# A two-block transformer forward pass on one core: a rebuilt front with one-number norms, row-wise memory and key/value products, and a new order of matmuls

## The reference, cut to what matters

```python
h = rmsnorm(x, norm_g)                               # per token
(a_q, a_ckv, i_q, i_k, i_w, a_gate, b_q, b_k, b_v, b_gate,
 c_q, c_gate, mix_gate) = split_cols(h @ w_in, IN_SIZES)
ckv = rmsnorm(a_ckv, kv_norm_g)                      # per token, width 256
a_k, a_v = split(ckv @ w_kv_up)
qa, ka = rmsnorm(a_q, q_norm_a), rmsnorm(a_k, k_norm_a)   # per token and head, 6 heads of 128
ik = layernorm(i_k, idx_k_ln_g, idx_k_ln_b)
oa = dsa_attention(qa, ka, va, iq, ik, iw, bias_a, topk) * silu(a_gate)
qb, kb = rmsnorm(b_q, q_norm_b), rmsnorm(b_k, k_norm_b)   # 12 and 2 heads of 64
ob = sliding_window_attention(qb, kb, vb, sinks_b, bias_b) * silu(b_gate)
m_k, m_v = split(rmsnorm(mem, mem_norm_g) @ w_mem_kv)
qc, kc = rmsnorm(c_q, q_norm_c), rmsnorm(m_k, k_norm_c)   # 4 heads of 128
oc = memory_attention(qc, kc, vc) * silu(c_gate)
x = x + (g_a*(oa@w_up_a) + g_b*(ob@w_up_b) + g_c*(oc@w_up_c)) @ w_o
# second block: rms_norm, w_in_2, pooling, conv, w_o_2, then square(relu(u @ w_up)) @ w_down
```

## Time and profile before

| | us |
|---|---|
| median of 3 runs | 2173.51 (2173.22 to 2175.52) |
| the profiled execution | 2172.68, span 2170.9 |
| TensorE matmuls busy | 2091.2 |
| TensorE weight loads busy | 1759.2 |
| VectorE busy | 1469.6 |
| ScalarE busy | 953.2 |
| GpSimd busy | 106.6 |
| chain that ended last: TensorE, VectorE, ScalarE | 89%, 7%, 2% of the span |

### The profile page before, as it was taken

The page is one execution under the profiler, slowest core; times in us unless marked ns, Lnnn a source line. Parts: engine busy times, 40 slices in busy tenths (PEclk is TensorE's granted clock), DMA queues, the critical chain, the costliest instruction groups (busy, mean ns, idle before and its releaser), DMA issues.

```text
span 2170.9 us, 29736 instructions
## 1 busy us (share of the span) xinstructions
PE 2091.2 (96%) x10683; PEld 1759.2 (81%) x10683; DVE 1469.6 (68%) x1877; ACT 953.2 (44%) x1185; POOL 106.6 (5%) x102
## 2 busy tenths in 40 slices
PE   6899999899999999999999999989999999999997
PEld 5777778777777888899878878878888888888886
DVE  6796886966676655567997757566556656645655
ACT  5443434545555444533444464454333333333343
POOL 4010010200100100001100000000000000000001
PEclk9999999999999999999999999999999999999998
DMA  7644555454655655555565646545565555556552
GB/s 242 196 123 127 165 155 166 138 171 161 192 165 180 231 190 182 180 169 171 164 194 190 189 147 233 192 145 186 192 194 184 188 194 181 191 194 193 184 194 87
DMA packets 272168, 386.59 MB, mean 178 GB/s; under 512 B 12247, under 2 KB 160565, under 8 KB 271527
## 3 DMA queue, kind: packets, MB, share of 16 engines
q1 hardware_dynamic: 267644, 370.91, 53.1%
q0 software_dynamic: 2208, 9.96, 1.3%
q10 hardware_dynamic: 2203, 4.23, 0.6%
HBM read 382.79 MB, written 2.13 MB: 177 GB/s over the span
## 4 chain that ended last, share of the span: by engine, by line
PE 89%; DVE 7%; ACT 2%; issue 1%; DMA 0%; SPq 0%; DVEq 0%; ACTq 0%
PE acc L492 17%; PE acc L494 17%; PE acc L493 17%; PE acc L513 17%; PE acc L512 8%; PE acc L505 2%; PE acc L503 2%; PE acc L504 2%; DVE w_low L444 2%; DVE rstd L1536 1%; PE acc L509 1%; PE aux L1218 1%; PE aux L1281 1%; ACT w_high L436 1%; PE acc L510 1%
## 5 line engine op out<-in xcount | busy, mean ns | idle before, releaser
L444 DVE TENSOR_TENSOR low_rows<-stage_rows,high_rows 128x1024 fp32r<-128x1024 f32 x416 | 512.3, 1235 | 398.4 <-ACT high_rows L436 394.5
L436 ACT ACTIVATE high_rows<-stage_rows 128x1024 fp32r<-128x1024 f32 x416 | 438.9, 1058 | 582.3 <-PE acc L494 547.7
L444 DVE TENSOR_TENSOR w_low<-stage,w_high 128x1024 fp32r<-128x1024 f32 (+1 forms) x294 | 357.1, 1223 | 231.0 <-ACT w_high L436 228.2
L436 ACT ACTIVATE w_high<-stage 128x1024 fp32r<-128x1024 f32 (+1 forms) x294 | 305.0, 1039 | 472.0 <-PE acc L513 364.3
L513 PE MATMUL acc<-u,w_high 128*128 128x512 f32 x960 | 342.4, 399 | 0.0
L512 PE MATMUL acc<-u,w_low 128*128 128x256 f32 x960 | 270.2, 281 | 0.0
L513 PE MATMUL acc<-hT,w_high 128*128 128x512 f32 x675 | 244.7, 400 | 0.0
L513 PEld LDWEIGHTS acc<-u,w_high 128*128 128x128 f32 x960 | 180.5, 188 | 41.8
L512 PE MATMUL acc<-hT,w_low 128*128 128x256 f32 x675 | 201.3, 298 | 3.9 <-DVE w_low L444 3.9
L492 PE MATMUL acc<-high_rows,f_pair 128*128 128x512 f32 x512 | 199.2, 389 | 0.0
L493 PE MATMUL acc<-low_rows,f_pair 128*128 128x512 f32 x512 | 199.2, 389 | 0.0
(11 more groups left out here) (359 smaller groups left out, 3521.5 us busy)
## 6 DMA issues: line engine op xcount, KB each, us to landing
stage_rows<-in_w_in SPq DMA_DIRECT2D x160, 512.0 KB, 3.6
stage<-in_w_in SPq DMA_DIRECT2D x136, 512.0 KB, 3.5
stage<-in_w_up SPq DMA_DIRECT2D x128, 512.0 KB, 3.9
stage_rows<-in_w_down SPq DMA_DIRECT2D x128, 512.0 KB, 4.3
stage_rows<-in_w_o SPq DMA_DIRECT2D x64, 512.0 KB, 3.5
stage<-in_w_mem_kv SPq DMA_DIRECT2D x16, 512.0 KB, 6.0
stage_rows<-in_w_pool_out SPq DMA_DIRECT2D x16, 512.0 KB, 3.5
stage_rows<-in_w_conv_out SPq DMA_DIRECT2D x16, 512.0 KB, 4.6
```

The lines of the kernel that those rows point to most:

```text
L436: act.activation(high[:, pr, 0:kt, 0:p.cols], src[:, slot, 0:kt, 0:p.cols], ACT.Copy).then_inc(high_done, 1)
L444: dve.tensor_tensor(low[:, pr, 0:kt, 0:p.cols], src[:, slot, 0:kt, 0:p.cols], high[:, pr, 0:kt, 0:p.cols].bitcast(F32), ALU.subtract).then ...
```

## The change

Five things are changed together.

1. `mem` and `x`. `mem_pair` and `hT` are made straight from `aux` (all four banks in turn): ScalarE writes the high part with the gain as scale (`high_unit`), VectorE the low part (`low_unit`). The first slab of `mem_kv` needs only unit 0; units 4 to 7 are turned beside slabs 0 to 3. Sums of squares are made by ScalarE from rows (`row_squares`, 2048 columns with an accumulator): `x` beside slabs 4 and 5, `mem` beside 7 and 12. `x` is scaled by VectorE in rows beside slabs 6 and 7, then turned beside slabs 8 to 11. SP loads `x` after slab 2 and the parameters after slab 4, and waits for a part of `mem` ahead of slab 1. The bias rows move from `mem_kv` to `early`, slabs 8 to 15.
2. `mem_kv`, `kv_up` and a new job `bkv` (key and value of the B heads) multiply by rows; ScalarE empties their banks with the norm of the token as scale. No value is turned any more; the keys are (`turn_keys`), after VectorE has scaled them (`scale_heads`).
3. Norms are one number per token and head (`rs`): sums by matmuls whose stationary operand is the squares and whose moving operand has one or two columns (`sum_steps`), or by ScalarE's accumulator (`head_squares`), then one `chain_var`, `chain_root`, `chain_inverse` for a batch. Query norms go into the logits, key and query gains into the turned keys.
4. The flips of the bias table move from `early` 7 to 15 to `late` 2 to 10.
5. By tiles, a group of four k does its low weights first, then its high weights.

The core of the diff:

```diff
@@ multiply
-                        both, a = p.rhs(k0 + k)
-                        if first:
-                            pe.matmul(bk, high, both, start=True, stop=False, skip_group_check=True)
-                            pe.matmul(bk[:, 0:T], low, a, start=False, stop=False, skip_group_check=True)
-                        else:
-                            pe.matmul(bk[:, 0:T], low, a, start=False, stop=False, skip_group_check=True)
-                            mm = pe.matmul(bk, high, both, start=False, stop=final, skip_group_check=True)
+                    opened = k0 == 0
+                    if opened:
+                        pe.matmul(bk, tile(w_high, 0), p.rhs(0)[0], start=True, stop=False, skip_group_check=True)
+                    for k in range(kt):
+                        pe.matmul(bk[:, 0:T], tile(w_low, k), p.rhs(k0 + k)[1], start=False, stop=False, skip_group_check=True)
+                    for k in range(1 if opened else 0, kt):
+                        mm = pe.matmul(bk, tile(w_high, k), p.rhs(k0 + k)[0], start=False, stop=last and k == kt - 1, skip_group_check=True)
@@ jobs
-            ("mem_kv", Job(4, [Part(A["w_mem_kv"], 0, full, rhs_of(mem_pair), ("pair_ready", 0))], 2)),
+            ("mem_kv", Job(2, [by_rows(A["w_mem_kv"], 0, [2] * 8, mem_pair, ("pair_ready", 0))], 2)),
-            ("kv_up", Job(6, [Part(A["w_kv_up"], 0, [2], rhs_of(ckv_pair), ("ckv_ready", 0))], 8)),
-            ("late", Job(14, [Part(A["w_in"], A_GATE, full, rhs_of(hT))], 2)),
+            ("kv_up", Job(3, [by_rows(A["w_kv_up"], 0, [2], ckv_pair, ("ckv_ready", 0))], 4)),
+            ("late", Job(6, [Part(A["w_in"], A_GATE, full, rhs_of(hT))], 2)),
+            ("bkv", Job(1, [Part(A["w_in"], B_KV_COL, full, None, rows=hT)], 2)),
+            ("late2", Job(7, [Part(A["w_in"], B_GATE_COL, full, rhs_of(hT))], 2)),
@@ steps
+        SQUARE_AT = {"early": {1: 0, 5: 1, 9: 2, 13: 3, 17: 4}, "late": {17: 5, 21: 6, 25: 7, 45: 8, 49: 9}}
+        FLIP_AT = 2
+        BIAS_AT = 8
-        SILU_AT = 52
+        SILU_AT = {48: 0, 50: 1, 52: 2}
@@ sync, the first slabs
+                    for n in range(2 * job.S):
+                        if n == 1:
+                            sp.wait_ge(s("mem_in1"), 16)
+                        load_slab(sp, job, 0, n // job.S, n % job.S)
+                        if n == 2:
+                            for c in range(4):
+                                cols = slice(c * 512, (c + 1) * 512)
+                                sp.dma_start(x_in[:, :, cols], xr[:, cols].rearrange("(t p) d -> p t d", p=P)).then_inc(s("x_in"), 16)
+                        if n == 4:
                             other_params()
@@ scalar
+            def high_unit(pair, gain, q, first):
+                act.wait_ge(s("turned_pe"), first + q + 1)
+                for a in range(2):
+                    k = 2 * q + a
+                    act.activation(pair[:, k, 0, :], aux[:, q % 4, a * T:(a + 1) * T], ACT.Copy, scale=column(gain, k)).then_inc(s("pair_high"), 1)
+            for q in range(4):
+                high_unit(mem_pair, "mem_norm_g", q, 0)
+                round_high(act, jobs["mem_kv"], 0, 0, q)
+            def beside_mem(n):  # parts
+                if n < 4:
+                    high_unit(mem_pair, "mem_norm_g", 4 + n, 0)
+                if n in (4, 5):
+                    row_squares(x_in, "x", n - 4, "input_squared")
+                if n == 6:
+                    chain_root(0)
+                if 8 <= n < 12:
+                    for q in (2 * (n - 8), 2 * (n - 8) + 1):
+                        high_unit(hT, "norm_g", q, 8)
+            def head_squares(kind, rows, width, t, h, total):
+                col = RS[kind] + t * total + h
+                if head_count[0]:
+                    act.wait_ge(s("head_squared"), head_count[0])
+                head_count[0] += 1
+                act.activation(junk_head[:, 0:width], rows[:, t, h * width:(h + 1) * width], ACT.Square, accum_out=sq[:, col:col + 1]).then_inc(s("head_squared"), 1)
+            def kv_body(i, u, part):
+                for t in range(2):
+                    act.activation(kv_rows[:, t, r * ROW:(r + 1) * ROW], banks[:, t, :], ACT.Copy, scale=rs_col("ckv", t)).then_inc(s("kv_rows"), 1)
@@ tensor
+                if 8 <= n < 12:
+                    if n == 8:
+                        pe.wait_ge(s("x_scaled"), 2)
+                        pe.wait_ge(s("params_copied"), 5)
+                    for q in (2 * (n - 8), 2 * (n - 8) + 1):
+                        turn_unit(x_in, q, 8)
+            def sum_steps(name, n):
+                i = stages(SQUARE_AT[name], n, 1)
+                kind, r = SQUARED[i]
+                pe.wait_ge(s("squared"), i + 1)
+                        else:
+                            c = base + t * (A_HEADS if kind == "aq" else C_HEADS) + 2 * r + a
+                            mm = pe.matmul(aux[:, 1, c:c + 1], v, ones[:, 0:1], start=True, stop=True)
+                if n == 4:
+                    pe.wait_ge(s("ik_diag"), 2)
+                if n in (5, 6):
+                    pe.wait_ge(s("ck_scaled"), 1)
@@ vector
+            def low_unit(pair, gain, q, first):
+                dve.wait_ge(s("pair_high"), 2 * (first + q) + 2)
+                for a in range(2):
+                    k = 2 * q + a
+                    link.put(dve.scalar_tensor_tensor(out=pair[:, k, 1, :], in0=aux[:, q % 4, a * T:(a + 1) * T], scalar=column(gain, k),
+                                                      in1=pair[:, k, 0, :].bitcast(F32), op0=ALU.mult, op1=ALU.subtract))
+            def beside_mem(n):  # parts
+                if n in (6, 7):
+                    if n == 6:
+                        chain_inverse(0)
+                    dve.tensor_scalar(x_in[:, n - 6, :], x_in[:, n - 6, :], rs_col("x", n - 6), None, ALU.mult).then_inc(s("x_scaled"), 1)
+                if n == 6:
+                    other_params()
+                if 9 <= n < 13:
+                    for q in (2 * (n - 9), 2 * (n - 9) + 1):
+                        low_unit(hT, "norm_g", q, 8)
```

More of the change, by code:

```diff
@@ L442, in subtract_low @@
             dve.wait_ge(high_done, n + 1)
-            src, high, low = (stage_rows, high_rows, low_rows) if p.rows else (stage, w_high, w_low)
+            src, high, low = (stage_rows, high_rows, low_rows) if p.by_rows else (stage, w_high, w_low)
             dve.tensor_tensor(low[:, pr, 0:kt, 0:p.cols], src[:, slot, 0:kt, 0:p.cols],
@@ L488, in multiply @@
                     first, final = k0 + k == 0, last and k == kt - 1
+                    high, low = (v[:, pr, k, 0:p.cols] for v in ((high_rows, low_rows) if p.by_rows else (w_high, w_low)))
                     for t in range(2):
-                        bk = acc[:, 2 * bank + t, :]
+                        bk = acc[:, 2 * bank + t, 0:p.cols]
                         x_high, x_low = (p.rows[:, k0 + k, half, t * P:(t + 1) * P] for half in range(2))
-                        pe.matmul(bk, x_high, high_rows[:, pr, k, :], start=first, stop=False)
@@ L493, in multiply, with tile @@
-                        pe.matmul(bk, x_high, low_rows[:, pr, k, :], start=False, stop=False)
-                        mm = pe.matmul(bk, x_low, high_rows[:, pr, k, :], start=False, stop=final)
+                        pe.matmul(bk, x_high, high, start=first, stop=False)
+                        pe.matmul(bk, x_high, low, start=False, stop=False)
+                        mm = pe.matmul(bk, x_low, high, start=False, stop=final)
                 for j in range(0 if p.rows else p.cols // P):
                     bk = acc[:, 2 * bank + j, :]
-                    for k in range(kt):
-                        first, final = k0 + k == 0, last and k == kt - 1
-                        high, low = (w[:, pr, k, j * P:(j + 1) * P] for w in (w_high, w_low))
-                        if p.width:
+                    def tile(w, k):
+                        return w[:, pr, k, j * P:(j + 1) * P]
@@ L501, in multiply @@
+                    if p.width:
+                        for k in range(kt):
+                            first, final = k0 + k == 0, last and k == kt - 1
                             a, b = p.rhs(k0 + k if p.stride else 2 * POOL_ORDER[u] + k)
                             dst = bk[:, 0:p.width]
-                            pe.matmul(dst, high, b, start=first, stop=False)
-                            pe.matmul(dst, low, a, start=False, stop=False)
-                            mm = pe.matmul(dst, high, a, start=False, stop=final)
@@ L754, in beside_mem @@
[L754 to L770 removed]
+                r = rstd[:, 0:T]
@@ L831, in silu_step, with bkv_body @@
+            def bkv_body(i, u, part):
+                banks, group = group_done(act, jobs["bkv"], 0, 0)
+                act.wait_ge(acc_free, 2 + group)
+                for t in range(2):
+                    act.activation(bkv[:, t, :], banks[:, t, 0:2 * P], ACT.Copy).then_inc(s("bkv_rows"), 1)
+                act.wait_ge(s("bkv_rows"), 2)
```

(8 more changed lines are left out.)

832 lines of the change are left out of this document (430 added, 402 removed).

## The result

The changed kernel takes 2118.47 us, median of 4 runs (2118.22 to 2118.83), the kernel before 2173.36 beside it: a ratio of 0.9747, 95% interval 0.973 to 0.9764. The profiled execution took 2118.83 us (span 2117.0), 53.9 less of span than before. The forecast was 2118.

What follows compares the result with a forecast made beforehand. TensorE is busy in 96% of the span, so only less TensorE work or fewer and shorter holes help; six parts sum to -54.5, taking 2172.7 to 2118 us, range 2108 to 2128 (chance 0.45).

Steps and rivals of the forecast that it cites:

- the order's terms: All groups by tiles: four low then four high matmuls save 0.022 us a group over 428 groups, 9.3 us.
- Part 1: Start to the first `early` product: 93.58 us becomes about 79, -14.6, with a new hole of 5 before `x`.
- Rival B: The start moves only its hole: `x` chain and VectorE subtractions hold `early` at 93.6; 2133 us, chance 0.15.
- Parts 2 and 3: `early`: waits, norms and flips go, sums and new holes come, -16.5; `kv_up`: three slabs in 8.5 us, -3.8.
- Parts 4 and 5: `late`: value waits, norms and value transposes go, flips and sums come, -8.0; behind it: `low_rows` waits shrink, -6.0.
- Part 6: Low x4, high x4 order saves 0.022 us a group: `w_up` -5.6, the other 172 groups 3.8.
- My own lower bound: Matmul order: a pair keeps its 0.353 and lows become 0.002 slower, +0.01 us a group.
- A: The matmul order is worth nothing, since the extra 4 ns of an alternating pair is contention that stays; 2127 us, chance 0.20.
- C: The matmul order is worth its bound, 428 x 0.028 more; 2106 us, chance 0.12.
- D: More of the front's waits come back: 38 steps between engines, each up to 0.7 late; 2145 us, chance 0.05.
- E: Slower: four 256-wide matmuls in a row cannot hide their weight loads, adding 90; 2218 us, chance 0.03.
- the deciding 0.155: Step in us of 256-wide matmuls in a row at which 1284 such steps eat the other parts' 49 us.

Runs made afterwards that it cites:

- keys apart: Changed kernel with the three key turns of the A heads beside slabs 6, 8 and 10 of `late` instead of 6, 7 and 8: 2114.76 us.
- the reciprocals at the end of `late`: Changed kernel with four idle VectorE reciprocals of 128x128 behind the other steps of each of slabs 45, 47, 49, 51, 53, 55 of `late`: 2126.67 us.
- alternation: Changed kernel with the matmuls of a group put back to low, high, low, high: 2121.35 us.
- runs of two: Changed kernel with low, low, high, high, low, low, high, high in a group: 2116.53 us.
- in eights: Changed kernel with the eight low matmuls of a slab first, then the eight high ones: 2116.96 us.

## Why the prediction was right, and where it was not

The total, -54.5 against -53.9 of span, is right by two errors. With the order's terms taken out, the forecast had -45.2 for everything else; measured are -51.4. For the order it had -9.3; measured are -2.4.

**Part 1** (-14.6; measured -16.6). First product at 14.57 for 13.6. `mem_kv` is 56.9 us for 59.3: slabs as forecast (step 0.228), turns dearer (four add 0.46 to a slab, 5.5 in all for 4.2), one hole of 2.55 before `x` for 5, and two waits not foreseen, 1.3 for the parameters' turn and 0.7. The low clock behind the hole cost 1.2 for 2.5. The low clock in the first slab, 2.5, did not come in this execution: its matmuls stand 0.23 us apart, behind sixteen small transposes and a wait of 2.2. In six of the twelve traces of the new front it did, in full (12 steps of 0.427 for 0.228, 2.4 us) or in part. That the profiled execution was one of the others is luck, worth about 1 us of the total, since the parameters' wait shrinks where the slab is slow. `ikw` took its 5.6. Slab 5 was late, as feared, but for ScalarE: the timeline of ScalarE after has

```profile
26.99 1.06 ACT L432 ACTIVATE high_rows<-stage_rows 128x1024 fp32r<-128x1024 f32 x1 [3.24 <-DMA stage_rows<-in_w_mem_kv]
...
32.94 1.94 ACT L724 ACTIVATE junk<-x_in 128x2048 f32<-128x2048 f32 x1
```

and no idle time between the two rows. TensorE, with slab 4 still to do, waited 0 to 0.45 us in the traces; the squares of `x`, in ScalarE's queue behind slabs 5 to 8, were pushed by it. It did not make the hole before `x`: ScalarE waits for TensorE once more at 38.31 us (0.51), ahead of the root, and the hole is 2.55 us too in the executions whose first slab came late. Rival B, `early` still at 93.6, is out.

**Parts 2 and 3** (-20.3 together, -18.9 without the order; measured -21.3). They must be judged together, since the boundary between them was misread by one slab. The sums cost 0.2 as taken. Of the new holes, `k_diag` came with 1.5 for 1.4; the wait before the first sum and the one for `ck_scaled` didn't. `kv_up` took 9.4 for 8.5: one wait for VectorE's fold is left, 0.9, where I had written that none would be. Before, it lasted 15.1 and not 12.3, with five holes of 0.9 to 1.2.

**Parts 4 and 5** (-14.0, -11.7 without the order; measured -13.3). `late` gained 4.6 and not 8.0, the slabs behind it 8.7 and not 6.0; some of that is the misread boundary. The step that failed in `late` is the next wait: I had named the key scaling beside top-k, about 1 us; it was the copy of the turned keys, twice 1.5, which keys apart removed. Behind `late` I had left 1.9 for the new chain of roots; it has no wait at all there. That a norm's reciprocal in VectorE's queue made the long wait is in the trace of the kernel before (436.93 us), and the reciprocals at the end of `late` show that a backlog put back there costs as much; with `w_up_a` as it was, the waits of 5.2 and the clock behind them are the 8.7 that it gained, so 2.7 for the clock was low and 1.9 for the roots too much.

**Part 6** (`w_up` -5.6, the other groups -3.8; measured -2.4 and nothing to be seen). The step that failed is the transfer of one number to another width. From 272 columns (12 ns over) and 512 (13 ns over, by rows) I took 13 to 14 ns for both widths in a run of its own. Measured in runs of four: 18.7 ns over for the wide, 11.4 for the narrow, where alternation has 22.3 and 10.8. Taken for each width, 13 to 14 over would have been 8 to 9 ns off a wide step and 2 to 3 more on a narrow one; measured are 3.6 off and 0.6 more. It is the wide ones that fell short. I had only the mean of both, 17, and did not see that alternation treats them so differently. My own lower bound (narrow ones slower by 2 ns) had the sign of the narrow ones. Nor does a wide one behind a wide one reach the 0.227 of the earlier trace rows in runs of two or four; it takes 0.231.

**Rivals.** A is out by the stage lengths, though its 0 was nearer to the order's worth than my 9.3; had the rest been as forecast, the time would have been 2125, close to A's 2127. C is out. D came true in part: 3.0 for keys, 1.3 and 0.7 for turns, but other waits that I had charged stayed away. E is out in its size: no run of narrow ones in `w_up` steps at more than 0.121, far from the deciding 0.155; whether loads set that step is open. Two of its sums were loose: 2118 + 90 is 2208, and 2218 stands only with the order's 9.3 taken back as well; the other parts had 45.2 us to lose and not 49.

What stays open: why the order gives 0.010 a group in `w_up` and nothing in `late` (186.13 us alternating, 186.35 in fours, 185.91 in twos, 185.76 in eights, each from one execution); why a row of narrow matmuls slows from its second step; why the clock falls behind the same wait in one execution and not in another; and 1 us of `mem_kv` that the terms above don't cover.

## What to carry to other kernels

Before summing stages, find each stage's first product by its operands, not by its wait. A wait on a chain whose result is needed slabs later is removed by moving the read one slab, and it can pay twice, since half clock stood behind the same wait of 2.55 us in seven traces of nine; when two products of one ring share a bank, leave a slab between them. When comparing single traces, check first what clock the first stage had in each. Order matmuls of unequal width in short runs and measure: here two and two beat alternation by 1.2%, and longer runs gave part of it back.

## What the runs showed of the hardware that I had not expected

- Matmuls that keep TensorE busy in the records can still lose the clock: behind 3.5 us of one-column fp32 products the windows show 0.74 and 0.83; behind 0.8 us of them 1.00.
- A one-column fp32 product costs 0.20 us start to start in a run of four and 0.22 in a run of twelve, about as much as 512 columns of fp32r (0.23).
- Programs that differ only behind the first slab run it at full clock in one execution and at 1.2 GHz in another (2.8 or 5.3 us), and the clock column can read 1.00 there while the steps are 0.427 us. Behind the wait for `x` the clock was 1.00 in two traces of nine and low in seven.
- In a run of matmuls of 256 columns the step rises from 0.1135 (first to second) to about 0.120 for the steps between, worked out from the means above; 512 columns take 0.2356 before a narrow one and about 0.230 before a wide one.
